# Value products of two attentions cut into quarters, and plain transposes in the banded one

## The chip, the cores and the metric

The kernel runs on one NeuronCore of a Trainium2 chip. The metric is the device time of one execution in microseconds, from launch to end; the span of the profile runs from the first to the last instruction. All arithmetic is in 32-bit floats: the large matrix products split their inputs into a rounded high part and a remainder; the attentions use the 32-bit form of TensorE directly.

## The reference, cut to what matters

Two models run one after the other on 512 tokens of width 1024 (with 256 context tokens in the first). Each has two layers. The change is in the two attentions of the first model: the banded one in layer 0 (8 heads of width 64, 2 key heads; each block of 128 queries sees the context, its own block and its two neighbours, with a sink logit per head), and the full one in layer 1 (8 heads of width 128, 2 key heads, context and all 512 tokens, no sink).

```python
def gqa_attend(q, k, v, sink=None):
    s = jnp.einsum('bqhgd,bkhd->bhgqk', q.reshape(b, tq, hkv, g, d), k) * d ** -0.5
    if sink is None:
        p = jax.nn.softmax(s, axis=-1)
    else:
        p = jax.nn.softmax(jnp.concatenate([s, s_sink], axis=-1), axis=-1)[..., :-1]
    o = jnp.einsum('bhgqk,bkhd->bqhgd', p, v)

def one_block(args):                                 # banded: one block of 128 queries
    s_win = jnp.where(valid_n, jnp.einsum('bqhgd,bkhd->bhgqk', qn, kn) * scale, -jnp.inf)
    s_ctx = jnp.einsum('bqhgd,bchd->bhgqc', qn, k_ctx) * scale
    p = jax.nn.softmax(jnp.concatenate([s_win, s_ctx, s_sink], axis=-1), axis=-1)
    o = (jnp.einsum('bhgqk,bkhd->bqhgd', p[..., :nw], vn)
         + jnp.einsum('bhgqc,bchd->bqhgd', p[..., nw:nw + n_ctx], v_ctx))
```

The context tokens of layer 0 use `gqa_attend` with the sink; layer 1 computes no output for the context.

## The kernel before

The program is a list of stages (`add(...)` at the end of `program`). Each stage hands one function to TensorE, ScalarE and VectorE; every engine runs its functions in the order written, and semaphores tie the engines together. Most stages, both attentions among them, end with a barrier of the three engines (L319). The great products of the layers (L497, L499) take most of the time; their weights come through a ring of four slabs by DMA, and VectorE and GpSimd split each slab in two. During the attentions the ring is full and those queues rest.

Both attentions are made by one function, `attention(groups, scale, p_at, pt_at, by_diagonal)`. A unit is one head of one block of 128 queries; four units that share a key head form a group and have one value product. The banded attention has 12 groups, 48 units: 16 units see two key tiles of 128 (the context's own blocks), 16 see four, 16 see five. In the program's order these are groups 0 to 3 with two tiles, 4 and 5 with four, 6 to 9 with five, 10 and 11 with four. The full attention has 8 groups, 32 units, all with six key tiles.

What happens to unit i, engine by engine:

- TensorE, `pe_fn`: the scores (L967 for the context's keys, L970 for the others) go to one of two pairs of PSUM banks. Two iterations later the probabilities are turned, tile by tile, into banks 4 and 5: in the banded attention by a matmul with a diagonal matrix that holds one over the row's sum (L992), so that it scales and turns at once, in the full attention by `transpose` with the identity (L994).
- VectorE, `dve_fn`: masks (L1006), maximum (L1009), minus the maximum (L1011 and L1012, or L1014); then, for the unit before, one over the sum (L1021, L1022) and either the diagonal (L1026) or, in the full attention, the scaled probabilities (L1028).
- ScalarE, `act_fn`: the exponential with the row's sum (L1042, L1043), then for unit i-2 the copy of the turned probabilities from PSUM to SBUF (L1054).
- The value product of a group (L979) multiplies the values with the turned probabilities of its four heads, 512 columns at once, one matmul for each key tile. It stands in TensorE's order in the iteration that issues the scores of unit i = 4g+6, between these and the turning of unit 4g+4, and it waits for the copy of the group's fourth head. ScalarE copies its result out in iteration 4g+7 (`put`, L1412 and L1446).

The order on each engine is the order of these loops; nothing reorders it. There are three buffers of probabilities, two of turned probabilities and two PSUM banks for products.

In the trace a 32-bit matmul shows two records, a transpose one. PE is TensorE's matmuls, PEld its loading of the fixed operand.

Of the kernel before, what the change touches and what calls it, by code (L numbers as in the profile page):

```python
# [225 lines left out]
def program(nc, xT_d, vec_d, shared_d, first_d, second_d, gup_d, sguw_d, sgub_d, crow_d, ada_d, w_d, out_d):  # L226
    with ExitStack() as ctx:
# [26 lines left out]
        PS = ctx.enter_context(nc.psum_tensor("PS", [P, 8, 512], F32))  # L254
# [679 lines left out]
        at_n, at_t, at_tc = signal("probs_normed"), signal("probs_turned"), signal("turned_probs_copied")  # L934
        at_o, at_oc = signal("head_outputs_ready"), signal("head_outputs_copied")

        def attention(groups, scale, p_at, pt_at, by_diagonal):
# [6 lines left out]
            n = len(units)  # L944
# [16 lines left out]
            def pe_fn(pe):  # L961
                for i in range(n + 3):
                    if i < n:
                        g, j = units[i]
                        if i >= 2:
                            pe.wait_ge(at_p.sem, at_p.at("pe", i - 2))
                        ins = pe.matmul(PS[:, 2 * (i % 2), 256:512], g["q"][j], g["k"][j][:, 0:CTX], start=True, stop=True)  # L967
                        if g["lat"]:
                            lo, hi = g["lat"]
                            ins = pe.matmul(PS[:, 2 * (i % 2) + 1, 0:hi - lo], g["q"][j], g["k"][j][:, lo:hi], start=True, stop=True)  # L970
                        ins.then_inc(at_s.sem, 1)
                    if i >= 3 and (i - 3) % 4 == 3:
                        gi, g = (i - 3) // 4, units[i - 3][0]
                        kts = key_tiles(g)
                        pe.wait_ge(at_tc.sem, at_tc.at("pe", i - 3))
                        if gi >= 2:
                            pe.wait_ge(at_oc.sem, at_oc.at("pe", gi - 2))
                        for t, kt in enumerate(kts):
                            ins = pe.matmul(PS[0:g["m"], 6 + gi % 2, :], g["v"](kt), turned[gi % 2][:, t, :],  # L979
                                            start=(t == 0), stop=(t == len(kts) - 1))  # L980
                        ins.then_inc(at_o.sem, 1)
                    if 2 <= i < n + 2:
                        u = i - 2
                        g, j = units[u]
                        kts = key_tiles(g)
                        pe.wait_ge(at_n.sem, at_n.at("pe", u))
                        if u >= 1:
                            pe.wait_ge(at_tc.sem, at_tc.at("pe", u - 1))
                        for t in range(len(kts)):
                            turned_ps, p_tile = PS[:, 4 + t // 4, (t % 4) * P:(t % 4) * P + P], probs[u % 3][:, t * P:t * P + P]  # L990
                            if by_diagonal:
                                ins = pe.matmul(turned_ps, p_tile, diag(u), start=True, stop=True)  # L992
                            else:
                                ins = pe.transpose(turned_ps, p_tile, C("ident"))  # L994
                        ins.then_inc(at_t.sem, 1)
                for s_, c_ in ((at_p, n), (at_n, n), (at_tc, n), (at_oc, len(groups))):
                    s_.advance("pe", c_)
# [36 lines left out]
            def act_fn(act):  # L1034
                for i in range(n + 4):
                    if i < n:
                        g, j = units[i]
                        act.wait_ge(at_nb.sem, at_nb.at("act", i))
                        if i >= 3:
                            act.wait_ge(at_t.sem, at_t.at("act", i - 3))  # L1040
                        if g["sinks"]:
                            nc.scalar.activation(col(i, 4), g["sinks"][j], ACT.Exp, bias=col(i, 2))  # L1042
                        nc.scalar.activation(probs[i % 3][:, 0:nk(g)], s_all(i, g), ACT.Exp, bias=col(i, 2), scale=scale,  # L1043
                                             accum_out=col(i, 3)).then_inc(at_p.sem, 1)
                    if 2 <= i < n + 2:
                        u = i - 2
                        g, j = units[u]
                        gi = u // 4
                        act.wait_ge(at_t.sem, at_t.at("act", u))
                        if j == 0 and gi >= 2:  # L1050
                            act.wait_ge(at_o.sem, at_o.at("act", gi - 2))
                        kt = len(key_tiles(g))
                        src = PS[:, 4:6, :].rearrange("p a b -> p (a b)")[:, 0:kt * P].rearrange("p (a b) -> p a b", a=kt)
                        nc.scalar.activation(turned[gi % 2][:, 0:kt, j * P:j * P + P], src, ACT.Copy).then_inc(at_tc.sem, 1)  # L1054
                    if i >= 4 and (i - 4) % 4 == 3:
                        gi, g = (i - 4) // 4, units[i - 4][0]
                        act.wait_ge(at_o.sem, at_o.at("act", gi))
                        g["put"](PS[0:g["m"], 6 + gi % 2, :].rearrange("p (h q) -> p h q", h=4)).then_inc(at_oc.sem, 1)
                at_nb.advance("act", n)
                at_t.advance("act", n)  # L1060
                at_o.advance("act", len(groups))
# [335 lines left out]
        def b_groups():  # L1397
            out = []
            for blk in range(NT):
                if blk < NCT:  # L1400
                    lat, masks = None, []
                else:
                    a, b = max(blk - 1, NCT), min(blk + 2, NT)
                    lat = (a * P, b * P)
                    masks = [(CTX + (t - a) * P, m) for t, m in ((blk - 1, "neg_ge"), (blk + 1, "neg_le")) if a <= t < b]
                for kv in range(2):
                    heads = [4 * kv + j for j in range(4)]
                    half = [64 * (h % 2) for h in heads]

                    def put(ps, kv=kv, blk=blk):  # L1410
                        for par in range(2):
                            ins = nc.scalar.activation(H[64 * par:64 * par + 64, 4 + 2 * kv:6 + 2 * kv, blk * P:blk * P + P],  # L1412
                                                       ps[:, par::2, :], ACT.Copy)
                        return ins

                    out.append(dict(q=[qb[o:o + 64, h // 2, blk * P:blk * P + P] for h, o in zip(heads, half)],
                                    k=[kd[o:o + 64, kv, :] for o in half], v=lambda kt, kv=kv: vb[:, kt, 64 * kv:64 * kv + 64],
                                    lat=lat, masks=masks, sinks=[V("sink", h) for h in heads], put=put, m=64))
            return out

        attn_b = attention(b_groups(), 64 ** -0.5, 3072, 18464, True)


        qc = area(0, 8, 512)
# [882 lines left out]
```

## Time and profile before

| | us |
|---|---|
| median of three runs | 4357.2 (4356.22 to 4358.87) |
| the profiled execution | 4357.44 |
| its span | 4355.6 |
| banded attention in it | 467.0 to 639.4 |
| full attention in it | 1408.6 to 1542.0 |

Over the span TensorE is busy 91% of the time, VectorE 51%, GpSimd 29%, ScalarE 18%; the mean granted clock of TensorE is 0.934 of its full rate. Half of the chain that ended last lies on the great products' line (L497). A profile is read here in two steps: the windows say how full each engine is in a stretch and at which clock TensorE ran; the timeline of one engine says what stands behind what, and, in brackets, how long the engine sat idle before an instruction and which instruction released it.

### The profile page before, as it was taken

The numbers are of one execution on the slowest core, as the hardware profiler recorded it, in microseconds if no ns is written. First come the engines' busy times: TensorE is split into PE (matmuls) and PEld (weight loads), VectorE is DVE, ScalarE is ACT, GpSimd is POOL, SyncE is SP. The second block draws the span as 40 slices with busy tenths as digits, with TensorE's granted clock in tenths as the row PEclk, the third lists the DMA queues.
The fourth block names the chain that finished last, engine by engine and source line by source line (L and its number), as shares of the span: only waits on it lengthen the run. The fifth ranks groups of instructions, "written<-read, shape, count | busy, mean of one in ns | idle before, by whom it ended". The sixth has DMA issues, their size and how long they took to land.

```text
span 4355.6 us, 45380 instructions
## 1 busy us (share of the span) xinstructions
PE 3966.4 (91%) x18926; PEld 3230.5 (74%) x18926; DVE 2239.5 (51%) x3645; ACT 781.6 (18%) x1462; POOL 1283.9 (29%) x522
## 2 busy tenths in 40 slices
PE   7976789999997889999999877999999999779998
PEld 5965459999985468888887745788788877457886
DVE  4824556876663462234347364733552473746334
ACT  3014432011122421100002222100100022221001
POOL 1310002333331034444443300444444433003443
PEclk9989899999998999999999956999999999569999
DMA  5410002344321012232222200222232222002222
GB/s 200 150 34 1 1 6 75 119 129 126 124 68 39 0 63 97 97 111 97 97 97 84 82 1 1 82 97 97 82 99 97 97 85 85 0 1 83 97 97 82
DMA packets 103695, 335.61 MB, mean 77 GB/s; under 512 B 11426, under 2 KB 11586, under 8 KB 103236
## 3 DMA queue, kind: packets, MB, share of 16 engines
q1 hardware_dynamic: 78192, 282.29, 19.4%
q10 hardware_dynamic: 25300, 50.43, 3.7%
q8 instruction: 150, 2.46, 0.2%
q14 instruction: 53, 0.43, 0.0%
HBM read 330.58 MB, written 2.10 MB: 76 GB/s over the span
## 4 chain that ended last, share of the span: by engine, by line
PE 59%; DVE 6%; ACT 2%; issue 1%; DVEq 0%; ACTq 0%
PE PS L497 50%; PE PS L979 1%; DVE XH L778 1%; PE PS L1861 1%; PE PS L499 0%; DVE H_r L655 0%; PE PS L1613 0%; PE PS L1614 0%; ACT arena L877 0%; PE PS L970 0%; PE PS L890 0%; PE PS L1864 0%; DVE small L1009 0%; PE PS L1631 0%; PE PS L2028 0%
## 5 line engine op out<-in xcount | busy, mean ns | idle before, releaser
L497 PE MATMUL PS<-arena_r,ring_hi 128*128 128x512 f32 (+1 forms) x6272 | 2120.4, 376 | 107.2 <-DVE H_r L655 102.3
L2220 POOL TENSOR_TENSOR ring_r<-ring,ring_hi 128x1024 fp32r<-128x1024 f32 x518 | 1283.7, 2479 | 3036.8 <-DVE ring_hi L337 3036.8
L497 PE MATMUL PS<-arena_r,ring_r 128*128 128x512 f32 (+1 forms) x4800 | 1800.9, 375 | 0.0
L497 PEld LDWEIGHTS PS<-arena_r,ring_hi 128*128 128x128 f32 x6272 | 1177.5, 189 | 291.5 <-issue 108.2
L497 PE MATMUL PS<-H_r,ring_hi 128*128 128x512 f32 (+1 forms) x3328 | 1249.9, 376 | 0.0
L497 PEld LDWEIGHTS PS<-arena_r,ring_r 128*128 128x128 f32 x4800 | 907.0, 189 | 132.9
L497 PEld LDWEIGHTS PS<-H_r,ring_hi 128*128 128x128 f32 x3328 | 632.4, 190 | 93.5 <-issue 0.5
L337 DVE CAST ring_hi<-ring 128x1024 fp32r<-128x1024 f32 x518 | 502.7, 973 | 276.1 <-DMA ring<-weights_dram 275.6
L1482 DVE SCALAR_TENSOR_TENSOR arena<-arena,PS 128x512 f32<-128x512 f32 x88 | 60.4, 687 | 447.3 <-PE PS L497 447.3
L1478 ACT ACTIVATE arena<-PS 128x512 f32<-128x512 f32 x88 | 52.6, 598 | 1073.5 <-PE PS L497 1073.5
L1093 DVE SCALAR_TENSOR_TENSOR XH<-PS,mods,XH 128x256 f32<-128x256 f32 (+1 forms) x144 | 68.5, 524 | 209.2 <-PE PS L497 209.2
L337 DVE CAST arena_r<-arena 128x512 fp32r<-128x512 f32 (+1 forms) x184 | 78.7, 428 | 176.2 <-ACT arena L1139 173.1
L1138 ACT ACTIVATE arena<-PS 128x384 f32<-128x384 f32 (+1 forms) x96 | 49.9, 520 | 610.8 <-PE PS L497 578.4
L1489 DVE SCALAR_TENSOR_TENSOR XH<-XH,PS 128x512 f32<-128x512 f32 x64 | 44.0, 687 | 223.1 <-PE PS L497 223.1
L1110 DVE TENSOR_TENSOR arena_r<-arena,arena_r 128x512 fp32r<-128x512 f32 (+1 forms) x184 | 118.8, 646 | 6.4
L655 DVE TENSOR_TENSOR H_r<-XH,arena_r 128x512 fp32r<-128x512 f32 (+1 forms) x144 | 113.9, 791 | 4.9
L544 DVE SCALAR_TENSOR_TENSOR rstd<-rstd,con 128x512 f32<-128x512 f32 x54 | 106.8, 1978 | 1.1
L1009 DVE TENSOR_REDUCE small<-PS 128x1 f32<-128x768 f32 (+3 forms) x80 | 61.6, 771 | 83.5 <-PE PS L970 60.7
L979 PE MATMUL PS<-arena 128*128 128x512 f32 (+1 forms) x184 | 90.2, 639 | 13.9 <-ACT arena L1054 13.8
L415 ACT ACTIVATE arena<-arena 128x512 f32<-128x512 f32 x48 | 29.5, 633 | 349.0 <-DVE arena L449 286.5
L778 DVE TENSOR_TENSOR XH<-XH,rstd 128x512 f32<-128x512 f32 (+1 forms) x80 | 71.9, 908 | 29.6 <-ACT mean L712 22.4
L337 DVE CAST arena_r<-XH 128x512 fp32r<-128x512 f32 (+1 forms) x144 | 71.6, 497 | 24.9 <-ACTq L319 22.7
(336 smaller groups left out, 3353.6 us busy)
## 6 DMA issues: line engine op xcount, KB each, us to landing
ring<-weights_dram SPq DMA_DIRECT2D x534, 512.0 KB, 3.3
rstd<-ada_later_dram ACTq DMA_DIRECT2D x54, 256.0 KB, 2.8
mean<-ada_later_dram ACTq DMA_DIRECT2D x53, 256.0 KB, 2.7
ada_extra<-ada_later_dram ACTq DMA_DIRECT2D x53, 256.0 KB, 2.8
XH<-xT_dram ACTq DMA_DIRECT2D x1, 3072.0 KB, 23.2
out_dram<-XH SPq DMA_DIRECT2D x8, 256.0 KB, 2.0
con<-second_dram ACTq DMA_DIRECT2D x1, 1536.0 KB
con<-first_dram ACTq DMA_DIRECT2D x1, 1280.0 KB, 7.9
```

Of the source, the lines that this page charges most:

```text
L337: return nc.vector.tensor_copy(out, src)
L497: ins = pe.matmul(PS[:, o.bank, 0:hi - lo], w[:, 0, :], x, **flags)
L544: return nc.vector.scalar_tensor_tensor(out=out, in0=w, scalar=1.0, in1=silu_rows[s][:, 512 * half:512 * half + 512], op0=ALU.mult, op1=AL ...
L655: nc.vector.tensor_tensor(H_r[:, k, lo:hi], x, x_hi.bitcast(F32), ALU.subtract).then_inc(xlo_ready.sem, 1)
L778: nc.vector.tensor_tensor(H[:, k, lo:hi], (H if centred else X)[:, k, lo:hi], root(i)[:, 0:hi - lo], ALU.mult).then_inc(norm_ready.sem, 1)
L979: ins = pe.matmul(PS[0:g["m"], 6 + gi % 2, :], g["v"](kt), turned[gi % 2][:, t, :], start=(t == 0), stop=(t == len(kts) - 1))
L1009: v_link(dve, nc.vector.tensor_reduce(col(i, 0), s_all(i, g), AX, ALU.max))
L1093: ins = nc.vector.scalar_tensor_tensor(out=X[:, m, a:b], in0=ps[:, a - lo:b - lo], scalar=mods[:, l, s, gate + m:gate + m + 1], in1=X[:, m ...
L1110: nc.vector.tensor_tensor(h_lo(lo, hi), h(lo, hi), h_hi(lo, hi).bitcast(F32), ALU.subtract).then_inc(hidden_ready.sem, 1)
L1478: a = ftile(x_x, LAT, "act", lambda eng, ps, lo, hi, m=m: nc.scalar.activation(h[:, m, :], ps, ACT.Silu))
L1482: return nc.vector.scalar_tensor_tensor(out=h[:, m, :], in0=h[:, m, :], scalar=0.5, in1=ps, op0=ALU.mult, op1=ALU.mult)
L2220: nc.gpsimd.tensor_tensor(ring_lo[:, slot, :, :], ring[:, slot, :, :], ring_hi[:, slot, :, :].bitcast(F32), ALU.subtract).then_inc(lo_read ...
```

## The change

The value product is cut: its key tiles are issued in four parts, in four iterations one after the other, each between the scores of unit i and the turning of unit i-2. The first part stands where the whole product stood, and only it waits for the copies; only the last part signals. A product of six tiles is cut into 1, 2, 1 and 2 tiles, of five into 1, 1, 1 and 2, of four into four, and of two into 0, 1, 0 and 1. The last group's product stays whole. ScalarE copies a group's result out three iterations later, the last group's where it was. The banded attention is built with `by_diagonal` False: VectorE scales each head's probabilities in place, 128 x 256 to 128 x 640 elements, and TensorE turns them with `transpose`.

```diff
--- before.py
+++ after.py
@@ -969,16 +969,20 @@
                             lo, hi = g["lat"]
                             ins = pe.matmul(PS[:, 2 * (i % 2) + 1, 0:hi - lo], g["q"][j], g["k"][j][:, lo:hi], start=True, stop=True)
                         ins.then_inc(at_s.sem, 1)
-                    if i >= 3 and (i - 3) % 4 == 3:
-                        gi, g = (i - 3) // 4, units[i - 3][0]
+                    if i >= 6:
+                        gi, quarter = (i - 6) // 4, (i - 6) % 4
+                        g = groups[gi]
                         kts = key_tiles(g)
-                        pe.wait_ge(at_tc.sem, at_tc.at("pe", i - 3))
-                        if gi >= 2:
-                            pe.wait_ge(at_oc.sem, at_oc.at("pe", gi - 2))
-                        for t, kt in enumerate(kts):
-                            ins = pe.matmul(PS[0:g["m"], 6 + gi % 2, :], g["v"](kt), turned[gi % 2][:, t, :],
+                        if quarter == 0:
+                            pe.wait_ge(at_tc.sem, at_tc.at("pe", 4 * gi + 3))
+                            if gi >= 2:
+                                pe.wait_ge(at_oc.sem, at_oc.at("pe", gi - 2))
+                        last = gi == len(groups) - 1
+                        for t in range(0 if last else len(kts) * quarter // 4, len(kts) if last else len(kts) * (quarter + 1) // 4):
+                            ins = pe.matmul(PS[0:g["m"], 6 + gi % 2, :], g["v"](kts[t]), turned[gi % 2][:, t, :],
                                             start=(t == 0), stop=(t == len(kts) - 1))
-                        ins.then_inc(at_o.sem, 1)
+                        if last or quarter == 3:
+                            ins.then_inc(at_o.sem, 1)
                     if 2 <= i < n + 2:
                         u = i - 2
                         g, j = units[u]
@@ -1052,8 +1056,9 @@
                         kt = len(key_tiles(g))
                         src = PS[:, 4:6, :].rearrange("p a b -> p (a b)")[:, 0:kt * P].rearrange("p (a b) -> p a b", a=kt)
                         nc.scalar.activation(turned[gi % 2][:, 0:kt, j * P:j * P + P], src, ACT.Copy).then_inc(at_tc.sem, 1)
-                    if i >= 4 and (i - 4) % 4 == 3:
-                        gi, g = (i - 4) // 4, units[i - 4][0]
+                    if i == n + 3 or (i >= 10 and (i - 10) % 4 == 0):
+                        gi = len(groups) - 1 if i == n + 3 else (i - 10) // 4
+                        g = groups[gi]
                         act.wait_ge(at_o.sem, at_o.at("act", gi))
                         g["put"](PS[0:g["m"], 6 + gi % 2, :].rearrange("p (h q) -> p h q", h=4)).then_inc(at_oc.sem, 1)
                 at_nb.advance("act", n)
@@ -1418,7 +1423,7 @@
                                     lat=lat, masks=masks, sinks=[V("sink", h) for h in heads], put=put, m=64))
             return out
 
-        attn_b = attention(b_groups(), 64 ** -0.5, 3072, 18464, True)
+        attn_b = attention(b_groups(), 64 ** -0.5, 3072, 18464, False)
 
 
         qc = area(0, 8, 512)
```

In the rows below, taken from the programs' order, the count behind x is that of equal instructions in a row. TensorE around a product of five tiles in the banded attention, before (L979 the product, L992 the turning by diagonals):

```order
L967 MATMUL PS<-arena 128x256
L970 MATMUL PS<-arena 128x384
L979 MATMUL PS<-arena 64x512 x5
L992 MATMUL PS<-scratch,arena 128x128 x5
L967 MATMUL PS<-arena 128x256
```

And in the changed kernel (L982 the product, L998 the transposes):

```order
L967 MATMUL PS<-arena 128x256
L970 MATMUL PS<-arena 128x384
L982 MATMUL PS<-arena 64x512
L998 MATMUL PS<-con,arena 128x128 x5
L967 MATMUL PS<-arena 128x256
L970 MATMUL PS<-arena 128x384
L982 MATMUL PS<-arena 64x512 x2
L998 MATMUL PS<-con,arena 128x128 x5
```

The block of five is gone; each head now has one or two matmuls of a product between its scores and the turning. The same place in the full attention, before:

```order
L967 MATMUL PS<-arena 128x256
L970 MATMUL PS<-arena 128x512
L979 MATMUL PS<-arena 128x512 x6
L994 MATMUL PS<-con,arena 128x128 x6
L967 MATMUL PS<-arena 128x256
```

and in the changed kernel:

```order
L967 MATMUL PS<-arena 128x256
L970 MATMUL PS<-arena 128x512
L982 MATMUL PS<-arena 128x512
L998 MATMUL PS<-con,arena 128x128 x6
L967 MATMUL PS<-arena 128x256
L970 MATMUL PS<-arena 128x512
L982 MATMUL PS<-arena 128x512 x2
L998 MATMUL PS<-con,arena 128x128 x6
```

The six matmuls of the product are spread over four heads as 1, 2, 1 and 2; the rest of the order is as it was.

## Rows read from the trace of the kernel before

**Rows 1.** Windows from:to, length; busy us (records) of each engine, PEclk, DMA, GB/s

```profile
467.00:639.40 172.40, 148.20 (x600) 85.16 (x600) 86.15 (x336) 75.11 (x216) 0.00 (x0) 0.92 0.00 1
1408.60:1542.00 133.40, 114.54 (x416) 62.73 (x416) 57.68 (x128) 58.46 (x104) 0.00 (x0) 0.95 0.00 1
514.00:628.00 114.00, 98.90 (x448) 59.45 (x446) 59.67 (x219) 50.53 (x130) 0.00 (x0) 1.00 0.00 1
1416.00:1528.00 112.00, 97.72 (x380) 54.54 (x380) 53.26 (x120) 52.39 (x95) 0.00 (x0) 1.00 0.00 0
472.00:482.00 10.00, 10.00 (x23) 5.40 (x24) 5.52 (x25) 4.56 (x19) 0.00 (x0) 0.50 0.01 2
```

**Rows 2.** Timeline, TensorE, banded attention: start, us, instruction; starts of value products

```profile
479.92 3.43 PE L979 MATMUL PS<-arena 128*64 128x512 f32 x4
...
490.04 1.93 PE L979 MATMUL PS<-arena 128*64 128x512 f32 x4 [0.31 <-ACT arena L1054]
...
509.20 3.67 PE L979 MATMUL PS<-arena 128*64 128x512 f32 x4
...
523.78 3.65 PE L979 MATMUL PS<-arena 128*64 128x512 f32 x8 [0.88 <-ACT arena L1054]
...
554.67 4.51 PE L979 MATMUL PS<-arena 128*64 128x512 f32 x10 [0.99 <-ACT arena L1054]
...
571.63 4.51 PE L979 MATMUL PS<-arena 128*64 128x512 f32 x10 [0.99 <-ACT arena L1054]
...
619.89 3.65 PE L979 MATMUL PS<-arena 128*64 128x512 f32 x8 [0.89 <-ACT arena L1054]
...
633.50 5.16 PE L979 MATMUL PS<-arena 128*64 128x512 f32 x8 [0.69 <-ACT arena L1054]
```

**Rows 3.** Timeline, TensorE, full attention: products, and one score product before one

```profile
1426.39 5.42 PE L979 MATMUL PS<-arena 128*128 128x512 f32 x12
...
1515.08 0.60 PE L967 MATMUL PS<-arena 128*128 128x256 f32 x2
...
1519.50 5.42 PE L979 MATMUL PS<-arena 128*128 128x512 f32 x12 [0.90 <-ACT arena L1054]
...
1534.17 7.16 PE L979 MATMUL PS<-arena 128*128 128x512 f32 x12 [0.90 <-ACT arena L1054]
```

**Rows 4.** Timeline, TensorE, full attention, behind a product: turning, scores, next scores

```profile
1431.64 0.82 PE L994 MATMUL PS<-con,arena 128*128 128x128 f32 x6
...
1432.30 0.60 PE L967 MATMUL PS<-arena 128*128 128x256 f32 x2
...
1434.24 0.60 PE L967 MATMUL PS<-arena 128*128 128x256 f32 x2
```

**Rows 5.** Timeline, TensorE, banded attention, heads of five tiles

```profile
549.76 0.70 PE L967 MATMUL PS<-arena 64*128 64x256 f32 x2
...
559.11 1.38 PE L992 MATMUL PS<-scratch,arena 128*128 128x128 f32 x10
...
560.42 0.70 PE L967 MATMUL PS<-arena 64*128 64x256 f32 x2
...
561.69 0.49 PE L992 MATMUL PS<-scratch,arena 128*128 128x128 f32 x2
```

**Rows 6.** Timeline, TensorE, banded attention, heads of two and four tiles

```profile
487.33 0.70 PE L967 MATMUL PS<-arena 64*128 64x256 f32 x2
...
519.62 0.70 PE L967 MATMUL PS<-arena 64*128 64x256 f32 x2
...
610.42 0.70 PE L967 MATMUL PS<-arena 64*128 64x256 f32 x2
...
611.48 0.71 PE L992 MATMUL PS<-scratch,arena 128*128 128x128 f32 x4
```

**Rows 7.** Groups by line and form, VectorE: scaling in the banded, the full attention

```profile
L1026 DVE TENSOR_SCALAR scratch<-con,small 128x128 f32<-128x128 f32 x48 | 13.8, 287 | 1.7
...
L1028 DVE TENSOR_SCALAR arena<-arena,small 128x768 f32<-128x768 f32 x32 | 19.9, 620 | 1.1
```

## Prediction

> **What bounds the kernel now.** I read the windows over the two stages first [rows 1]: in the banded attention (467.0 to 639.4 us, 172.4 long) TensorE is busy 148.2 us, VectorE 86.2, ScalarE 75.1; in the full attention (1408.6 to 1542.0, 133.4 long) 114.5, 57.7 and 58.5. TensorE is the fullest engine but leaves 24 and 19 us idle, and its busy time also counts pipeline ends and stretches at half clock. GpSimd and the DMA queues do nothing in either, so a shorter stage uncovers no transfer. Nothing outside the two stages changes; the whole prediction is what these two lose.
>
> Then the starts of the value products [rows 2, 3]: they give the period of a group of four heads, and they show each product as one solid block. Three steps fill a head on TensorE: S (scores), T (turning the probabilities), and O (its share of the product). Between blocks the heads go round a chain: S(i), maximum on VectorE, exponential of i and then copy of the turned head i-2 on ScalarE, T(i-1), S(i+2). So TensorE waits for ScalarE where no product is queued, while during the block the other two engines run dry. Both happen in every group.
>
> **Part 1: quarters, full attention.** Behind a block TensorE runs from a stock of ready heads without a wait, and the starts there give its own pace [rows 4]: T at 1431.64, next S at 1432.30, next S at 1434.24. T costs 0.66 us (six tiles, 0.11 each), S 1.28, a head 1.94. The block takes 1426.39 to 1431.64 = 5.25. A group thus needs 4 x 1.94 + 5.25 = 13.0 us of TensorE; the period is (1519.50 - 1426.39) / 6 = 15.52 [rows 3]. Six tiles fall into quarters of 1, 2, 1, 2, that is 0.88 or 1.75 us.
>
> Is the chain covered when a quarter stands in each head? The last S before a block starts at 1515.08, and the copy that its chain ends in lets the block start at 1519.50 [rows 3]: 4.4 us from S(i) to the point where T(i-1) may start. TensorE has, between these two points, S(i) 1.28, a quarter, T 0.66, S(i+1) 1.28 and the next quarter: 3.2 + 0.88 + 1.75 = 5.8. Only where i+1 is a first quarter, which waits for that same copy, is it 3.2 + 1.75 = 4.95. Both exceed 4.4: no wait is left, and the period becomes 13.0. Six periods save 6 x 2.5 = 15.1. The last one, 1519.50 to 1534.17 = 14.67, now runs: first quarter and T 1.54; S, second quarter, T 3.7; third quarter and T 1.5; fourth quarter and T 2.4; copy and latency 1.1; together 10.2, saving 4.5. Sum **19.6 us**. The last product stood partly at half clock (7.16 us for what takes 5.42 elsewhere [rows 3]); with TensorE denser before it, that may go, worth up to 1.7; I count 0.4. Ends: 15 (a third of the covered waits come back) and 22.
>
> **Part 2: plain transposes.** The 176 tiles (16 heads each of 2, 4 and 5) go through as two records each now (x10 for five tiles [rows 5]) and as one each then (x6 for six [rows 4]). The trace shows both kinds: T of five tiles by diagonals 559.11 to 560.42 = 1.31 us [rows 5]; by transposes six tiles took 0.66 [rows 4]. Five tiles then cost 0.55 to 0.66, the upper end because T, S and O here have different shapes and each change of shape shows about 0.1 us (the product of ten, 4.44 to the next start, against 4.30 for ten of 0.43). I take 0.66, 0.55 and 0.33 for five, four and two tiles. S is 560.42 to 561.69 = 1.27 with five tiles [rows 5], 610.42 to 611.48 = 1.06 with four [rows 6]; with two an estimate of 0.63, half of that and a change of shape.
>
> VectorE: 48 scalings of a 128 x 128 diagonal at 287 ns become scalings of 128 x 256 to 128 x 640. Bounds: 287 ns and the 620 ns of 128 x 768 in the other stage [rows 7]; on the line between them 0.35, 0.49, 0.55. That adds 0.07 to 0.27 us a head, 8.6 in all, to an engine busy half the time. Nobody waits for it where the chain above rules: T(u) asks for the scaling of u one whole head after the chain has moved on. It costs up to 0.1 us a head in the two-tile heads, where VectorE needs 1.5 us a head against a pace of about 1.55; counted there. The diagonal's wait for an earlier T falls away; ScalarE waits for the same T before, so nothing is won.
>
> **Part 3: quarters, banded attention.** The chain by rows: S at 549.76, the copy lets the product start at 554.67: 4.91 us for five tiles; S at 519.62 to the product at 523.78: 4.16 for four; 487.33 to 490.04 = 2.71 for two [rows 2, 5, 6]. A five-tile group needs of TensorE 4 x (1.27 + 0.66) + 4.44, and 0.14 for each of three more changes of shape: 12.6. Between S(i) and T(i-1) it has 5.2 us with quarters of one tile, enough for 4.91, but a little less across an edge of groups; I add 0.3: 12.9 instead of 16.96 [rows 2]. The product's intervals from start to start, before and after, by the same sum with each interval's own heads:
> 479.92 to 490.04: 10.1, 7.8 (starts at half clock). To 509.20: 19.2, 13.6 (two groups; chain 2.7 + 0.33 for two heads). To 523.78: 14.6, 9.6 (chain 4.16 + 0.55 for two heads). To 554.67: 30.9, 23.7. To 571.63: 17.0, 12.9. To 619.89: 48.3, 36.8 (three groups). To 633.50: 13.6, 8.3 (no scores left, as in part 1).
> Sum 153.6, 112.7: 40.9 less. Before the first product some 1 us more, and the last one perhaps at full clock: **42 us**. Ends: 30, if each change of shape costs 0.2 more and a 0.3 us wait stands at each head of the larger groups, and 46.
>
> A check from the other side: the full-clock work after is 16 x (0.96 + 1.61 + 1.93) for S and T, 39.5 for the products and 5 for changes, 116.5 us in a stage of 130: 90% full, high but no more than the other stage comes to (104 of 113).
>
> **Moved steps.** The group's output copy goes three heads later on ScalarE, behind the copy of head i-2 and ahead of an exponential that has 1.2 us or more of slack there (0.6 or 0.75 us of work): nothing. The second bank and buffer of a pair are reused only after that: the first quarter of group g+2 asks for the copy of g, issued four heads before: nothing.
>
> **Sum.** 4357.4 (the profiled execution, 0.2 over the median of three) - 19.6 - 0.4 - 42 = 4295.4; I say 4296.
>
> **Rivals.**
> *Half clock, the slower side.* The granted clock is 0.50, the 1.2 GHz level, in 472 to 482, and 1.00, 2.4 GHz, in 514 to 628 and in 1416 to 1528 [rows 1]; before it rose TensorE had turned by diagonals and then run a solid product. Both of these go. If the banded stage stayed at 1.2 GHz, its work of 116.5 us would take 1.8 times as long (the product of four is 3.43 at one level and 1.93 at the other [rows 2]): 210, with start and end 218, 46 us more than now; less 20 in the other stage: **4383**. It decides once about 77 of the 116 us run low (77 x 0.8 = 62, the whole gain). Against it: in 1416 to 1528 a fifth of the work is transposes and the clock stayed at 1.00 [rows 1].
> The Trainium skill ("TensorE: Matmul & The Clock Gate", Part 4: PE-mode transpose) says that the full clock "doesn't engage" for transposes. By that rule the banded stage could stay low, the case just priced; the trace of the other stage does not agree with it where products stand between them. 3%.
> *Low only through the two-tile heads.* There the work is thinnest (the chain of 3.0 us against 2.9 of work for two heads). Held at 1.2 GHz up to the fourth product, these intervals take 10.7, 21 and 11 us: 12 more, **4308**. 17%.
> *No overlap.* If the quarters lie in the chain and not beside it (each waits on what the chain delivers), the full attention keeps 4 x 2.6 + 5.2 = 15.5, its present period, and the banded stage wins only half a microsecond or so for each two heads, some 13 us: **4344**. For it: the first quarter does wait on the chain. Against: the other three don't. 8%.
> *The cuts cost what they win.* If each of the three further cuts of a product costs not the 0.1 us of a change of shape but 0.5, as after an empty queue, 18 groups pay some 25 us: 4320. Against: S to T in the full attention shows no gap at all, 1.94 = 1.28 + 0.66 [rows 4]. 6%.
>
> **How the numbers follow.** Forecast 66% (4284 to 4305), the others as given. The range that leaves out no more than 2 in 10 is 4282 to 4322: below it is only both upper ends together, above it no overlap and the slow case. A difference under 0.2%, 8.7 us, is about what a measurement of this kernel can't tell from none. All cases but the half clock (slower, 3) are faster by more, save a tail of no overlap whose 13 us shrink under 8.7 (2): 95, 2 and 3 in 100.
>
> **What would show it.** Product starts 13.0 us apart in the full attention, and in each head a piece of the product between scores and transposes, without a wait for a copy; periods of 12.6 to 13 in the five-tile part; the transposes at 0.11 us a tile; granted clock 1.00 from the first four-tile heads on. It is wrong if TensorE shows waits for the turned copy in the later quarters, if the maximum's wait for scores shrinks but the one of T for the scaling grows, or if the clock is 0.50 for longer than now.

## The result, and the profile after

| | before | changed |
|---|---|---|
| median, us | 4357.58 (4356.22 to 4358.87, 4 runs) | 4311.43 (4310.36 to 4312.39, 4 runs) |
| span of the profiled execution | 4355.6 | 4308.6 |
| banded attention, first score to VectorE's first step behind it | 172.5 | 146.1 |
| full attention, likewise | 133.4 | 111.4 |

The ratio of the changed kernel's time to the other's is 0.9895, with a 95% interval of 0.9882 to 0.9909: 46 us faster, where 61 were forecast. The two stages lost 26.4 and 22.1 us; the sum, 48.5, is 1.5 more than the spans differ by. The full attention won a little more than forecast (20), the banded one 16 less than its 42. The time lies within the stated range, but above the forecast's own 4284 to 4305 us: it is that of a rival, as the clock below shows.

Windows over the changed kernel, columns as in [rows 1]; the first ends 1.6 us behind the stage:

```profile
467.70:615.40 147.70, 139.44 (x424) 61.00 (x424) 96.25 (x340) 75.02 (x216) 0.00 (x0) 0.83 0.00 1
1384.30:1495.70 111.40, 106.99 (x416) 62.45 (x416) 57.76 (x129) 59.84 (x104) 0.00 (x0) 0.98 0.00 1
467.70:470.00 2.30, 0.70 (x4) 0.30 (x4) 1.35 (x6) 0.53 (x2) 0.00 (x0) 1.00 0.00 0
472.00:520.00 48.00, 47.34 (x94) 18.86 (x94) 26.98 (x111) 21.75 (x77) 0.00 (x0) 0.50 0.00 1
522.00:608.00 86.00, 83.39 (x307) 38.42 (x306) 65.13 (x215) 49.22 (x127) 0.00 (x0) 1.00 0.00 1
```

In the banded stage TensorE is now busy 139 of 148 us where it was 148 of 172 [rows 1], in the full one 107 of 111 where it was 114.5 of 133.4. But the granted clock, 1.00 at the first scores, is 0.50, 1.2 GHz, in 472 to 520. In the kernel before it was at that level in 472 to 482 [rows 1], for some 7 us around 510, and for a few us ahead of the last product. The second of these, from the kernel before:

```profile
507.00:514.00 7.00, 7.00 (x17) 3.12 (x16) 2.55 (x11) 2.19 (x7) 0.00 (x0) 0.52 0.00 0
```

The mean over the stage fell from 0.92 to 0.83.

The pieces of the value products in the banded stage (L982), as in [rows 2]; x2 is one key tile:

```profile
481.00 1.97 PE L982 MATMUL PS<-arena 128*64 128x512 f32 x2
...
486.43 1.97 PE L982 MATMUL PS<-arena 128*64 128x512 f32 x2
...
491.87 1.97 PE L982 MATMUL PS<-arena 128*64 128x512 f32 x2
...
517.44 1.97 PE L982 MATMUL PS<-arena 128*64 128x512 f32 x2
...
523.49 1.07 PE L982 MATMUL PS<-arena 128*64 128x512 f32 x2
...
527.11 1.07 PE L982 MATMUL PS<-arena 128*64 128x512 f32 x2 [0.38 <-ACT arena L1058]
...
551.57 1.07 PE L982 MATMUL PS<-arena 128*64 128x512 f32 x2 [0.61 <-ACT arena L1058]
...
560.48 1.93 PE L982 MATMUL PS<-arena 128*64 128x512 f32 x4
...
564.30 1.07 PE L982 MATMUL PS<-arena 128*64 128x512 f32 x2
...
609.32 3.65 PE L982 MATMUL PS<-arena 128*64 128x512 f32 x8 [0.69 <-ACT arena L1058]
```

The first two are the two pieces of the first group, 491.87 is the first of the second group (10.9 us for a two-tile group at 1.2 GHz), 517.44 and 523.49 are those of the fourth. The fifth group's first piece, at 527.11, stands where the product at 523.78 stood [rows 2]. The stage began 0.7 us later here, so up to this point it lost 2.6 us against the kernel before, where the forecast had it win 14. Behind it all goes as forecast: 82.2 us from there to the last product (109.7 before), with 81.7 in the prediction. A five-tile period is 564.30 - 551.57 = 12.7 us, for 16.96 [rows 2] and a forecast of 12.9; the only wait left in it is that of its first piece for ScalarE's copy, 0.6 us. The last product runs at full clock, 3.65 us for 5.16 [rows 2].

One head of five tiles in that stage: piece of product, transposes, scores, next piece.

```profile
541.98 1.07 PE L982 MATMUL PS<-arena 128*64 128x512 f32 x2
542.99 0.77 PE L998 MATMUL PS<-con,arena 128*128 128x128 f32 x5
543.68 0.70 PE L967 MATMUL PS<-arena 64*128 64x256 f32 x2
...
544.95 1.07 PE L982 MATMUL PS<-arena 128*64 128x512 f32 x2
```

The full attention, as in [rows 3]: the second piece of two products, two groups apart, and the last product.

```profile
1430.16 1.88 PE L982 MATMUL PS<-arena 128*128 128x512 f32 x4
...
1456.04 1.88 PE L982 MATMUL PS<-arena 128*128 128x512 f32 x4
...
1489.57 5.42 PE L982 MATMUL PS<-arena 128*128 128x512 f32 x12 [0.90 <-ACT arena L1058]
```

The period is (1456.04 - 1430.16) / 2 = 12.94, forecast 13.0, before 15.52. The last product is at 5.42 us.

VectorE's scalings in the banded stage, as in [rows 7]; the line between two rows had given 0.55, 0.49 and 0.35 us:

```profile
L1032 DVE TENSOR_SCALAR arena<-arena,small 128x640 f32<-128x640 f32 x16 | 8.9, 553 | 0.6
...
L1032 DVE TENSOR_SCALAR arena<-arena,small 128x512 f32<-128x512 f32 x16 | 7.8, 486 | 0.6
...
L1032 DVE TENSOR_SCALAR arena<-arena,small 128x256 f32<-128x256 f32 x16 | 5.7, 353 | 0.6
```

### The profile page after: what moved, and what is told of

It is laid out like the page before. It is cut to its first block, busy times and chain, and to the rows that moved or that the text cites. A ratio compares the mean times of both kernels' runs of the same rounds, so it can differ in the third digit from the quotient of the medians.

```text
span 4308.6 us, 44983 instructions
## 1 busy us (share of the span) xinstructions
PE 3953.8 (92%) x18750; PEld 3209.2 (74%) x18750; DVE 2247.4 (52%) x3645; ACT 783.0 (18%) x1462; POOL 1284.7 (30%) x522
## 4 chain that ended last, share of the span: by engine, by line
PE 60%; DVE 5%; ACT 2%; issue 0%; DVEq 0%; ACTq 0%
PE PS L497 51%; PE PS L982 1%; DVE XH L778 1%; PE PS L970 1%; PE PS L1866 1%; PE PS L499 0%; PE PS L998 0%; PE PS L1618 0%; PE PS L1619 0%; ACT arena L877 0%; PE PS L1869 0%; DVE H_r L655 0%; PE PS L1636 0%; PE PS L890 0%; PE PS L2033 0%
## 5 line engine op out<-in xcount | busy, mean ns | idle before, releaser
L337 DVE CAST arena_r<-arena 128x512 fp32r<-128x512 f32 (+1 forms) x184 | 78.7, 428 | 175.6 <-ACT arena L1144 172.5
L982 PE MATMUL PS<-arena 128*128 128x512 f32 (+1 forms) x184 | 98.0, 639 | 3.2 <-ACT arena L1058 3.2
L998 PEld LDWEIGHTS PS<-con,arena 128*128 128x128 f32 x368 | 42.9, 148 | 64.3 <-issue 46.7
```

Of the source, the lines that this page charges most:

```text
L337: return nc.vector.tensor_copy(out, src)
L982: ins = pe.matmul(PS[0:g["m"], 6 + gi % 2, :], g["v"](kts[t]), turned[gi % 2][:, t, :], start=(t == 0), stop=(t == len(kts) - 1))
```

## The experiments

The question after the result was not where the 46 us came from, which the forecast had, but why TensorE stayed at 1.2 GHz through the two-tile heads, where it worked almost without a pause. Each kernel's time stands against runs of the kernel before on the same chip. The groups of experiments ran on different chips, where the kernel before took 4354 to 4358 us, so two kernels of different groups are compared by their ratios to it. Only one execution of each kernel has a trace.

### Each part alone

The changed kernel, with the diagonals kept in the banded attention:

```diff
-        attn_b = attention(b_groups(), 64 ** -0.5, 3072, 18464, False)
+        attn_b = attention(b_groups(), 64 ** -0.5, 3072, 18464, True)
```

> Quarters in both attentions, the banded one still turning by diagonals (two records a tile). The granted clock of the changed kernel is 0.50 up to 520 us, where the kernel before had 1.00 from 483 us. Theory A, the transposes keep it low: here it rises before 490 us; TensorE's work in the banded stage is then 16 x (1.27 + 2.15 + 2.58) + 44 = 140 us, the stage about 150 (172.4 before, 146.1 changed), the time about 4313. Theory B, it was the solid product that raised it, and cutting it keeps the clock low: 0.50 to about 515 us here too, the stage about 160, the time about 4323.

Measured: 4327.9 us, ratio 0.9929 (0.9901 to 0.9957). The six executions fall in two groups, 4309 to 4317 and 4339 to 4341. The profiled one is of the second; its windows:

```profile
470.00:540.00 70.00, 70.00 (x166) 38.54 (x165) 29.31 (x126) 25.36 (x86) 0.00 (x0) 0.50 0.00 1
550.00:640.00 90.00, 89.16 (x391) 49.84 (x390) 49.34 (x183) 44.26 (x112) 0.00 (x0) 1.00 0.00 1
```

For 70 us TensorE worked without a pause, at 1.2 GHz, with diagonal matmuls in every head; the stage took 176.8 us. So the clock can stay low without any transposes, later even than theory B had it (to about 543 us). That does not rule theory A out: the three shorter executions fit its 4313 us better than theory B's 4323. Their mean granted clock is on record, 0.935, 0.935 and 0.932 against 0.928 in the three longer ones. Between 0.935 and 0.928 lie some 65 us at 1.2 GHz, an estimate from clock and span, which at the 1.8 of the two product times [rows 2] makes 29 us, the difference between the groups. That these 65 us lie in the banded stage is an assumption; no trace of the shorter executions was kept. Cut products leave the moment of the rise open, in one and the same kernel.

The kernel before, with the transposes and VectorE's scaling alone:

```diff
-        attn_b = attention(b_groups(), 64 ** -0.5, 3072, 18464, True)
+        attn_b = attention(b_groups(), 64 ** -0.5, 3072, 18464, False)
```

> The kernel before with plain transposes and the scaling on VectorE in the banded attention, all products whole. Theory A: clock 0.50 until the four-tile heads (about 515 us), the stage about 170, the time about 4355. Theory B: the clock rises behind the first solid product, near 483 us, the chain of two heads is 0.3 to 0.65 us shorter, the stage about 159, the time about 4344.

Measured: 4366.9 us, ratio 1.0022 (1.0013 to 1.0031): slower than before, which neither theory had. Windows over one group of five-tile heads, and its product in the timeline:

```profile
554.00:558.00 4.00, 4.00 (x11) 2.15 (x10) 2.47 (x8) 1.66 (x4) 0.00 (x0) 0.50 0.00 0
558.00:562.00 4.00, 4.00 (x8) 1.24 (x8) 2.48 (x8) 1.07 (x3) 0.00 (x0) 0.73 0.00 0
562.00:566.00 4.00, 4.00 (x18) 2.00 (x16) 0.45 (x2) 0.70 (x1) 0.00 (x0) 1.00 0.00 0
566.00:570.00 4.00, 2.30 (x12) 1.35 (x11) 3.69 (x14) 2.36 (x7) 0.00 (x0) 1.00 0.00 0
570.00:574.00 4.00, 4.00 (x11) 2.37 (x12) 2.68 (x10) 1.91 (x6) 0.00 (x0) 0.55 0.00 0
574.00:578.00 4.00, 4.00 (x6) 1.08 (x5) 2.79 (x9) 1.97 (x5) 0.00 (x0) 0.50 0.00 0
```

```profile
557.94 5.60 PE L979 MATMUL PS<-arena 128*64 128x512 f32 x10
```

The product starts at 557.94 at half clock, and the clock rises while it runs; the heads behind it run at 2.4 GHz from their stock, then TensorE waits for the chain (2.3 us busy in 566 to 570), and the clock is gone within 1 us of 570. This goes on through the whole stage: mean clock 0.72 over 475 to 640, the stage 184.9 us for 172.5. With diagonals the same heads held 1.00 from 514 to 628 [rows 1]. So the clock rises while a solid product runs (theory B), and in these heads, which wait for the chain, it falls with transposes and not with diagonals. Whether that is the transposes' kind, or that they are half the records, these runs don't separate; in the full attention before, transposes and waits went with 1.00 for 112 us [rows 1]. Alone, this part of the change costs 10 us.

Quarters in the full attention alone (the banded one as before, its output copies too):

```diff
-                        last = gi == len(groups) - 1
+                        last = gi == len(groups) - 1 or g["sinks"] is not None
...
-        attn_b = attention(b_groups(), 64 ** -0.5, 3072, 18464, False)
+        attn_b = attention(b_groups(), 64 ** -0.5, 3072, 18464, True)
```

> Quarters in the full attention alone; the banded attention is that of the kernel before. Both theories: the banded stage 172.4 us, the full one 111 (133.4 before), product starts 12.9 us apart, the time about 4335. If the full attention's gain were partly given back behind it, the time would be above 4338.

Measured: 4334.5 us, ratio 0.9947 (0.9932 to 0.9961), the full stage 111.3 us. As both theories had it: 22 us, and nothing of them is given back. Its banded stage took 170.7, and began 4 us later than in the kernel before; some us of that kind lie between any two of these profiles, so differences of 3 us between kernels are not read here.

| banded attention, stage in us | products whole | products cut |
|---|---|---|
| diagonals | 172.5 (before) | 176.8 in the profiled execution; 23 to 30 less in three others, estimated from their times |
| transposes | 184.9 | 146.1 (changed) |

Transposes alone lose. Cut products alone, where the clock came up early, reached what both parts reach (4309 to 4317 us for 4310 to 4312); where it did not, they won nothing in this stage. The changed kernel, with both parts, had the short stage in all four of its executions, by their times. That the transposes save time beside cut products which run at full clock is not shown.

### Where the clock rises and where it falls

The products of the four two-tile groups whole, in the place of their first quarter, the rest as changed:

```diff
-                        last = gi == len(groups) - 1
+                        last = gi == len(groups) - 1 or not g["lat"]
+                        if last and quarter:
+                            kts = []
-                        if last or quarter == 3:
+                        if quarter == (0 if last else 3):
```

> The changed kernel, but the products of the four groups with two key tiles stay whole, in the place of their first quarter; transposes throughout. Theory A: clock 0.50 up to about 515 us as in the changed kernel, the time about 4311. Theory B: the clock rises behind the first product, near 483 us, and the two-tile groups take 8 us each instead of 10.9: about 10 us less, 4301.

Measured: 4307.0 us, ratio 0.9883 (0.9866 to 0.9899), not clear of the changed kernel's. Windows:

```profile
470.00:515.00 45.00, 40.71 (x89) 15.77 (x90) 25.80 (x109) 20.13 (x76) 0.00 (x0) 0.62 0.00 1
528.00:605.00 77.00, 75.78 (x276) 34.85 (x276) 58.28 (x192) 44.30 (x115) 0.00 (x0) 1.00 0.00 1
```

This lies between the theories: the clock rises with each product and falls again, a mean of 0.62 up to 515 us; the stage is 145.4 us, 0.7 shorter than the changed kernel's, which is too little to read.

Only the first group's product whole (the other lines as in the kernel above):

```diff
+                        last = gi == len(groups) - 1 or (not g["lat"] and gi == 0)
```

> The changed kernel with only the first group's product whole (two key tiles). With all four two-tile products whole the clock rose behind each and fell again between them. Theory C, a solid product raises it and cut products hold it, as they do from 522 us on in the changed kernel: 1.00 from about 483 us on, three two-tile groups at 6.4 instead of 10.9 us and a faster start of the four-tile ones, the time about 4296. Theory D, two-tile heads turned by transposes can't hold it, whatever stands between: it falls within one group, 0.50 to about 515 us again, the time 4308 to 4312.

Measured: 4310.3 us, ratio 0.9893 (0.9879 to 0.9908).

```profile
484.00:490.00 6.00, 4.89 (x15) 1.89 (x14) 2.70 (x13) 2.42 (x9) 0.00 (x0) 0.78 0.01 3
491.00:520.00 29.00, 28.67 (x57) 11.62 (x56) 15.32 (x61) 13.26 (x46) 0.00 (x0) 0.50 0.00 0
526.00:605.00 79.00, 76.92 (x284) 36.08 (x284) 60.18 (x198) 45.31 (x117) 0.00 (x0) 1.00 0.00 1
```

This is theory D: raised at about 485 us, the clock was gone by 489 and stayed low for 30 us. Cut products and transposes do not hold it in two-tile heads, though they hold it in the larger ones.

The two-tile heads wholly as before, diagonals and whole products (the second pair of lines stands in TensorE's and in VectorE's function):

```diff
+                        last = gi == len(groups) - 1 or not g["lat"]
...
-                            if by_diagonal:
+                            if not g["lat"]:
```

> The changed kernel, with the two-tile heads wholly as before (diagonals and whole products). In the kernel before the clock held 1.00 from 483 to 507 us with these. Theory D: it does so here, the product of the fourth group starts near 508 us (the changed kernel's fifth starts at 527, this one's near 521), the time about 4305. Theory C gives the same clock; if it does not hold here either, the diagonals are not what holds it, and the time is 4311 or more.

Measured: 4312.8 us (4308.5 to 4320.4), ratio 0.9901 (0.9886 to 0.9916).

```profile
485.00:507.00 22.00, 18.12 (x74) 9.94 (x73) 13.67 (x63) 12.01 (x45) 0.00 (x0) 1.00 0.00 1
509.00:514.00 5.00, 5.00 (x9) 1.40 (x9) 2.08 (x7) 1.30 (x5) 0.00 (x0) 0.50 0.00 0
521.00:532.00 11.00, 10.90 (x25) 5.05 (x26) 5.93 (x20) 4.77 (x14) 0.00 (x0) 0.53 0.01 1
```

The diagonals hold it, as theory D had it, from 485 to 507; but it falls then, as in the kernel before, and a second time by 521, soon after the transposes begin. Nothing is won: 4305 was wrong, by 8 us.

TensorE's idle time ahead of both attentions filled with matmuls whose result nobody reads, and one more such matmul behind the first two heads' scores:

```diff
+                for _ in range(3 if d == 64 else 4):
+                    pe.matmul(PS[:, 7, :], C("ident"), C(f"cos{d}", 0, 512), start=True, stop=True)
...
+                        if i == 2:
+                            pe.matmul(PS[:, 7, :], C("ident"), C("cos64" if g["sinks"] else "cos128", 0, 512), start=True, stop=True)
```

> The changed kernel with matmuls of no use (identity times a table, into a bank that is free) in TensorE's idle time ahead of both attentions and one behind the first two score products: 3 x 2 and 4 x 2 records of 512 columns ahead, 1 x 2 within. Theory C: the clock is 1.00 when the heads begin and holds, the banded stage 146 - 17 = 129 us, the full one 109, the time about 4290. Theory D: it falls in the first two-tile group, the banded stage stays at 145, only the full one wins 2 us: 4308.

Measured: 4305.8 us (4305.4 to 4316.5), ratio 0.9891 (0.9875 to 0.9908).

```profile
452.00:464.00 12.00, 7.57 (x22) 3.27 (x20) 6.61 (x11) 1.64 (x4) 0.00 (x0) 1.00 0.00 0
466.00:515.00 49.00, 48.28 (x94) 18.99 (x94) 27.58 (x114) 21.64 (x79) 0.00 (x0) 0.50 0.00 1
520.00:605.00 85.00, 81.74 (x301) 37.90 (x302) 62.79 (x207) 48.94 (x127) 0.00 (x0) 1.00 0.00 1
```

The clock is 1.00 when the heads begin (463.5 us), and 0.50 2 us later, for 50 us, as theory D had it. But it tells less than it was meant to: in the changed kernel too the clock is 1.00 at the first scores (467.70 to 470.00 above) and lost behind them. The ratio is not clear of the changed kernel's; what the trace shows won lies ahead of the heads (the matmuls that double the keys take 2.85 us at 2.4 GHz for 5.49), not in them.

The two-tile groups last:

```diff
-            for blk in range(NT):
+            for blk in [*range(NCT, NT), *range(NCT)]:
```

> The changed kernel with the groups of the banded attention in another order: the eight with four and five key tiles first, the four with two tiles last. It separates the kind of head from the place. Theory C (a stretch without a solid product doesn't raise it): the clock stays at 0.50 for tens of us from the start, through four- and five-tile heads now, at twice their work: 4315 or more. Theory D (it is the two-tile heads): 1.00 from about 475 us on through the larger heads, lost at the end with the two-tile ones: 4300 to 4306.

Measured: 4297.7 us (4292.2 to 4299.3), ratio 0.9862 (0.9847 to 0.9877), the banded stage 133.2 us.

```profile
475.00:490.00 15.00, 14.84 (x37) 8.94 (x38) 9.68 (x35) 6.75 (x19) 0.00 (x0) 0.50 0.00 1
492.00:583.00 91.00, 89.62 (x324) 40.40 (x322) 67.57 (x232) 51.64 (x140) 0.00 (x0) 1.00 0.00 1
585.00:604.00 19.00, 15.28 (x49) 5.50 (x48) 11.51 (x51) 11.80 (x45) 0.00 (x0) 1.00 0.00 1
```

The time is that of theory D, or better; the course of the clock is neither theory's. It is up 22 us after the first scores (at 493 us) instead of 53, where theory D said 475 us; and the two-tile heads at the end run at 1.00, where theory D had them lose it, though TensorE is busy only 15.3 of 19 us there. So two-tile heads don't lose the clock wherever they stand. This is the shortest median of all the kernels, with a ratio clear of the changed kernel's (59 us below the kernel before, where that was 46).

### Can the first 22 us be had too?

That order, and the first group's product whole:

```diff
+                        last = gi == len(groups) - 1 or (g["sinks"] is not None and gi == 0)
```

> Groups with two key tiles last, as in the kernel that took 4297.7 us, and the first group's product (four key tiles, eight records) whole. There the clock rose 20 us after the heads began, behind the first cut pieces of product (491 us). If a solid product raises it sooner: at once behind it, which at half clock ends some 7 us after it starts, so about the same moment (492 to 496 us): 4297 to 4300. If cut products keep it low longer in other executions (there the runs spread over 4292 to 4299), the spread shrinks.

Measured: 4305.5 us (4304.6 to 4305.8), ratio 0.9886 (0.987 to 0.9903).

```profile
475.00:487.00 12.00, 11.84 (x28) 6.37 (x28) 8.30 (x28) 5.37 (x15) 0.00 (x0) 0.50 0.01 1
490.00:495.00 5.00, 4.06 (x18) 2.18 (x16) 2.56 (x10) 1.86 (x5) 0.00 (x0) 1.00 0.00 0
498.00:515.00 17.00, 17.00 (x34) 7.14 (x34) 9.28 (x31) 5.90 (x15) 0.00 (x0) 0.50 0.00 0
520.00:605.00 85.00, 81.57 (x288) 35.19 (x286) 63.74 (x235) 52.39 (x157) 0.00 (x0) 1.00 0.00 1
```

That is 5.5 us above the range given. The clock rises at about the same time after the first scores (23 us for 22), and the heads behind the product then empty the stock: TensorE is busy 4.06 of 5 us, the clock falls at 496 us, and 20 more us go by at 0.50. This early rise ahead of a wait was worth nothing.

That order, products cut, and the filled idle time (the edits of both kernels above together):

> The same order, products cut, and TensorE's idle time ahead of both attentions filled with useless matmuls. With two-tile heads first the filled clock was lost again at 465 us, and the gain was 5.6 us over the changed kernel (5 ahead of and around the stages, 0 in the two-tile heads). If the larger heads hold a high clock from the start: the first 20 us at half clock go, about 7 us, and 3 to 5 us ahead of the two stages: 4286 to 4289. If they lose it too in the first heads, where the chain has not filled yet: 4292.

Measured: 4299.6 us (4299.1 to 4300.4), ratio 0.9873 (0.9859 to 0.9888).

```profile
470.00:475.00 5.00, 3.09 (x14) 1.67 (x14) 3.19 (x11) 1.79 (x6) 0.00 (x0) 1.00 0.01 2
477.00:495.00 18.00, 17.44 (x42) 8.81 (x41) 10.87 (x36) 7.97 (x23) 0.00 (x0) 0.50 0.00 1
500.00:600.00 100.00, 95.81 (x341) 42.02 (x341) 75.93 (x274) 60.67 (x179) 0.00 (x0) 1.00 0.00 1
```

The first heads wait for the chain, which has yet to fill (3.09 of 5 us busy), and lose the clock. That is the second branch of the expectation, which had 4292: 8 us too little. The ratio is not clear of that of the same order without the filling.

The order, the filling and the first product whole together:

> Both together: filled idle time, two-tile heads last, the first product whole. No more than the better of the two if the clock is already high when the product comes (4286 to 4289, and 0.5 us more for the product that lies in the chain); 4290 if it is low there and the product raises it.

Measured: 4300.8 us (4300.6 to 4301.4), ratio 0.9876 (0.9862 to 0.9891). The clock is 0.50 in 470 to 485, rises with the whole product and falls again (0.50 in 496 to 502), as without the filling. The case with a low clock at the product had 4290, so it too was wrong, by 11 us.

Two-tile groups last, and five-tile heads ahead of the four-tile ones:

```diff
+            for blk in (NCT + 1, NCT + 2, NCT, NCT + 3, *range(NCT)):
```

> Two-tile heads last again, and the larger heads in another order: five, four, four tiles (blocks 3 and 4, then 2 and 5, then the context's). With four-tile heads first the heads began at 471 us and the clock rose at 491, 20 us later, in the first pieces of a product. If the rise comes the sooner the more work a head has for TensorE: at once or within 14 us, 3 us or so won, 4294. If it comes only when pieces of a product join the heads, whatever the heads: the same moment after the first piece, which stands 21 us behind the start with five-tile heads at half clock, 4298 to 4300.

Measured: 4304.4 us (4297.2 to 4304.7), ratio 0.9879 (0.9862 to 0.9895).

```profile
475.00:503.00 28.00, 28.00 (x62) 13.55 (x62) 16.70 (x56) 10.45 (x26) 0.00 (x0) 0.50 0.00 1
505.00:600.00 95.00, 92.55 (x332) 41.07 (x331) 70.89 (x258) 56.05 (x168) 0.00 (x0) 1.00 0.00 1
```

Both readings fall in the profiled execution: with more work in each head the clock rose 36 us after the first scores, not 22, and 15 us behind the start of the first piece, while TensorE was busy all of 28 us. Three executions took 4304.3 to 4304.7 us, the fourth 4297.2. What sets the moment at which the clock rises among cut products, 22, 36, 53 or 77 us after the first scores, these runs don't tell. It may in part be a matter of the execution and not of the kernel, as in the kernel with diagonals and cut products.

## Why the prediction was right or wrong

**Part 1 was right, step by step.** TensorE's own pace of 1.94 us a head and 5.25 a product, the chain covered by quarters with room, so no wait: the period was 12.94 for 13.0. The stage won 22.1, for 20.0 counted. The periods and the last interval won the 19.6 of the sum; the last product's return to full clock won 1.7, counted with 0.4; and 0.7 fell ahead of the first product, not counted. The kernel with this part alone shows 22 us over the whole time.

**Part 2, the costs, was right.** A five-tile head runs piece at 541.98, transposes 542.99, scores 543.68, next piece 544.95: 1.01, 0.69 and 1.27 us. The forecast had 0.89 for a piece with 0.14 for a change of shape, 0.66 and 1.27. VectorE's scalings take 353, 486 and 553 ns, as on its line. TensorE's matmuls never wait for them in the larger heads.

**Part 3 was right from the fifth group on** (82.2 us for 81.7) **and wrong before it.** The step that failed is the one that wrote 7.8, 13.6 and 9.6 us for the intervals up to the fifth product, at full clock but for a few us. From the first score of the stage to the fifth group's first piece the forecast comes to 43 us, the trace shows 59.4: 16 us, which is the whole miss of the stage. The mechanism that failed is the clock, which the forecast took as high there: it named "1.00 from the first four-tile heads on", whose scores begin at 505 us, and called itself wrong "if the clock is 0.50 for longer than now". Both signs went against it, and the time is in the range only because the range took in a rival. The rival "low only through the two-tile heads" had named this and put the time at 4308; the result is 3 us above. It got 17%, and the prediction gives no reason for so little. The trace of the kernel before held what spoke for it: the rise came while a solid product ran, which the change cuts, and the clock fell again around 510 us, in the same kind of heads, although they were turned by diagonals.

**The half-clock rival** was too strong as a whole, but what carries it was not far off: with the transposes alone the kernel before is slower by 10 us, through the clock. The Trainium skill's sentence ("TensorE: Matmul & The Clock Gate", Part 4: PE-mode transpose) that the full clock "doesn't engage" for transposes fits that kernel in part: the clock fell between its products, where diagonals held it; but transposes with pieces of product between them ran at 1.00 for 86 us in the changed kernel, so as it stands the trace does not agree. The two other rivals are out: the later quarters wait for nothing, and a cut costs 0.15 us, not 0.5 (1.01 x 3 + 1.86 = 4.89 us for a five-tile product, 4.44 before).

**The check from the other side** gave 116.5 us of full-clock work in 130. Its sum is right, and it could not see the miss, since it also took the clock as given.

## What to carry to other kernels

When a change takes work from TensorE or spreads a solid block, ask of each stretch at which clock it will run, not only how long its instructions are: in the banded stage the same two edits gave -26 us together and +12 for the transposes alone, and the cut alone +4 in the execution with a trace and about -18 to -26 in three others, by their times. Cutting a product so that it stands between steps of a chain paid here what TensorE's own pace says, where a piece stood in every step and the clock was high. And try the thinnest work where the clock is already up, not at the start: with the four thin groups at the end the gain over the kernel before was 59 us where it had been 46, and 49 to 55 in the four other kernels with these groups at the end, which had more edits.

## What the runs showed that I had not expected

- TensorE can be busy without a pause by the records, 70 of 70 us, and stay at 1.2 GHz (diagonals with cut products), or 47 of 48 in the changed kernel. The same kernel on the same chip took 4309 us in one execution and 4341 in another.
- A clock raised early was lost within a few us where TensorE then waited for the chain: 3.1 to 4.1 us busy of 5 in the windows before each fall, and yet 15.3 of 19 held it at the end of the stage with the two-tile groups last.
